# Two mixture-of-experts starts, the hand-over between experts, and the compressed attention branch, rearranged in one kernel

## The chip, the cores and the metric

The kernel runs on one core of one Trainium2 chip. The metric is the device time of one execution in microseconds (us). Most executions of one kernel agree within 0.3%.

Names: PE is TensorE (matmuls; PEld is its weight load), DVE is VectorE, ACT is ScalarE, POOL is GpSimd and SP is SyncE, whose queue issues the loads of weights. A name with a q (PEq, DVEq) is that engine's instruction queue.

## The reference, cut to what matters

Two transformer blocks of two layers each on 256 tokens of width 1024, all in f32. The first block has a gMLP and latent attention mixer, then an NSA mixer (native sparse attention), each followed by a hierarchical mixture of 32 experts (hidden width 256). The second block has two hybrid mixers, two cross attentions, one dense feed-forward and one mixture of 8 experts with hidden width 2816. The parts that matter here:

```python
def compress_kv(k, pos_emb, w1, w2):            # S=256 tokens, G=2 groups, D=64
    blocks = ...                                 # 15 blocks of 32 tokens, stride 16, + pos_emb
    return gelu(flat @ w1) @ w2                  # w1: 2048 x 256, w2: 256 x 64

def nsa_compressed(q, k_cmp, v_cmp):             # 16 heads, 8 of a group; 15 compressed keys
    s = einsum('btgid,bngd->bgitn', q, k_cmp) * D ** -0.5
    p = where(mask, softmax(where(mask, s, NEG)), 0.0)
    return einsum('bgitn,bngd->btgid', p, v_cmp)
# later: o = gates[0] * o_cmp + gates[1] * o_slc + gates[2] * o_win

def moe(x):                                      # top 2 of n experts for each token
    y = sum_e weight_e * (silu(x @ w_gate[e]) * (x @ w_up[e])) @ w_down[e]
```

## The kernel before, in words

**Weights.** SP loads all weights in the order of a plan into a ring of 9 tiles of 1 MB (`weight_ring`); a tile is asked for when the one nine before it was used (`ring.used`). Where a product needs more than one pass of rounded f32, a tile is split in two: ACT rounds it into one of three buffers (`weights_high`, `HIGHS = 3`), which takes one ACTIVATE of 128x2048, and DVE leaves the rest in the ring (`leave_low`, one TENSOR_TENSOR of 128x2048). PE then forms `high*high + high*low + low*high` (`three_products`, L129 to L131) or two products (L1887).

**Stages.** Every engine runs its own list, written out by hand. `join()` (L186) ends a stage: each engine drains, raises a semaphore and waits for the other three. Nothing behind a join starts before it.

**The NSA mixer** (`nsa_mixer`). `projection` runs ten products, the last four of them the queries. After the join DVE builds the blocks for keys and values (16 instructions, L1168) and the gate logits (L1174), PE multiplies them with `w1` (L1188), ACT takes the gelu (L1209), PE multiplies with `w2` (L1194, L1197, L1201), DVE copies the results to SBUF, and a join follows. Then come 32 score matmuls, one for each head and half of the tokens, each with 64 rows and 15 columns (L1234), the softmax on DVE and ACT (L1243 to L1260), and for each of four pairs of token half t and group g: 8 transposes (one for each head, 128x15), a copy of 15x1024 by DVE (L1291), 8 matmuls of 15 rows and 64 columns (L1280) and a multiplication with the gates (L1294). A join ends the branch.

**A mixture of experts** (`sparse_experts`, run three times: twice with 32 small experts, once with 8 large ones of 11 chunks each). `split_rows` splits the token rows into two buffers of `weights_high`. DVE makes the 0/1 matrix `G`, which also lies in `weights_high` (buffer 0), and the weighted one, `GW`. PE turns `G` (L2225), gathers the rows of all slots in 8 products k = 0..7 into the 8 banks of PSUM (L2233), and DVE takes the even and ACT the odd ones to SBUF (L2250, L2262). Then PE sums the weights of the slots (L2241, 16 matmuls of one column), DVE copies the sums (L2254), and a join follows. Only behind it does ACT round the first tile, since all three buffers of `weights_high` are in use before.

**Small experts** (`SmallExperts`). ACT and DVE run `scalar_step` and `vector_step` for x = -3, -2, ...; step x splits the second tile of expert x+2 and the first of x+3, and makes the two halves of the window of x+3 (the columns of its slots; L2014 on ACT, L2060 on DVE). PE's first product is L1887.

**Large experts** (`SplitExpert`). For each expert PE runs two first products (gate and up) for each chunk j and one down product; the hidden rows are turned (L1599), rounded by ACT (L1698) and left low by DVE (L1718) before the down product. ACT and DVE follow `order()`, whose `part(j)` is L1698 on ACT and L1718 on DVE. The end of an expert in both lists reads

```python
        self.order(lambda q: self.low(dve, q, i), combine, part,
                   lambda q: next_window and self.low(dve, q, i + 1))
        self.used(dve, self.p0 + self.down(self.chunks - 1), i)
        nc.vector.tensor_copy(self.rows[:, 512:], c.psum[:, 5, :])...
        if next_window:
            next_window()
            self.low(dve, self.up(0), i + 1)
```

where `next_window` makes the window of the next expert: 128x1024, L1680 on ACT and L1684 on DVE. PE turns the output rows (L1634) and starts the next expert when L1684 is done.

Of the kernel before, what the change touches and what calls it, by code (L numbers as in the profile page):

```python
# [1079 lines left out]
def nsa_mixer(c, cat, ctx, ahead):  # L1080
# [12 lines left out]
    hid = sb("hid", [P, 2, CMP_HID // P, NSA_G * NCMP])  # L1093
    w2 = sb("w2", [P, 2, CMP_HID // P, NSA_D])
    kc = sb("kc", [P, NSA_G * NCMP])
    vc = sb("vc", [NCMP, NSA_G, NSA_D])
# [4 lines left out]
    pcT = c.xT[0:NCMP].rearrange("p (a k) t -> p a (k t)", a=2).rearrange("p a (h q) -> p a h q", q=P)  # L1101
    sc = sb("sc", [P, TT, NSA_H, NCMP])
# [3 lines left out]
                    (w2[:, 0], k_tiles(arg["c_w_ck2"][0])), (w2[:, 1], k_tiles(arg["c_w_cv2"][0]))] +  # L1106
                [(pos[a * 64:(a + 1) * 64, i, :], posv[a, :, i, :]) for a in range(2) for i in range(2)])

    @c.block.gpsimd
    def _(pool):  # L1110

        nc.gpsimd.memset(ends[:, :, :], 0.0)
        nc.gpsimd.memset(block_rows[:, CMP_LEN * at_j:], 0.0)
        nc.gpsimd.memset(vs[:, :, NSA_KV:], 0.0)
        nc.gpsimd.memset(vwg[:, :, NSA_KV + 3 * NSA_H:], 0.0)
        c.pool(nc.gpsimd.memset(ends01[:, :, :], 1.0))
        pool.drain().then_inc(*c.sig("blocks_padded").up())
        for t in range(TT):
            for m, fill in ((ends, NEG), (ends01, 0.0)):
                nc.gpsimd.affine_select(out=m[:, t, :], in_=m[:, t, :], compare_op=ALU.is_ge, fill=fill,  # L1120
                                        base=t * P - CMP_LEN + 1, pattern=[[-CMP_STRIDE, NCMP]], channel_multiplier=1)
    w_in = arg["c_w_in"][0]
# [15 lines left out]
    def input_low(dve):  # L1138
        dve.wait_ge(*high.at(1))
        nc.vector.tensor_tensor(parts[1], c.xT[:, :, :], c.xh[:, :, :].bitcast(F32), ALU.subtract).then_inc(*c.sig("input_split").up())  # L1140
    projection(c, [
# [8 lines left out]
        Cols(parts, w_in, at(4), NSA_KV, "dve", spread(3, nc.vector.tensor_copy))] + [  # L1150
        Cols(parts, w_in, j * 256, 256, "dve" if j % 2 else "act",
             (dve_copy if j % 2 else act_copy)(qT[:, 2 * j:2 * j + 2, :])) for j in range(4)])
# [3 lines left out]
    built, hidden, squashed, compressed = c.sig("blocks_built"), c.sig("cmp_hidden"), c.sig("cmp_squashed"), c.sig("cmp_ready")  # L1156

    @c.block.vector
    def _(dve):
        dve.wait_ge(*c.sig("mixer_params_landed").now())  # L1160
        for i in range(2):
            for a in range(2):
                h = slice(a * 64, (a + 1) * 64)
                for g in range(NSA_G):
                    src = kvT[h, i, g, :].rearrange("p (m r) -> p r m", r=CMP_STRIDE)
                    for half in range(2):
                        js = slice(half * 8, half * 8 + 8)
                        last = nc.vector.tensor_tensor(  # L1168
                            blocks[h, i, js, g, :], src[:, a:CMP_STRIDE:2, half:half + NCMP],
                            pos[h, i, js].unsqueeze(2).broadcast_to([64, 8, NCMP]), ALU.add)  # L1170
            dve.drain().then_inc(*built.up())

        for t in range(TT):
            last = nc.vector.tensor_tensor(gates[:, t, :], vwg[:, t, NSA_KV:NSA_KV + 3 * NSA_H], gate_b[:, :], ALU.add)  # L1174
        dve.drain().then_inc(*built.up())

    @c.block.tensor
    def _(pe):
        pe.wait_ge(*c.sig("blocks_padded").now())
        pe.wait_ge(*c.sig("mixer_params_landed").now())  # L1180
        pe.wait_ge(*built.at(2))
# [11 lines left out]
        for m in range(2):  # L1193
            last = nc.tensor.matmul(c.psum[0:64, 4, 0:NSA_G * NCMP], w2[:, 0, m, :], hid[:, 0, m, :], start=(m == 0), stop=(m == 1))  # L1194
        last.then_inc(*compressed.up())
        for m in range(2):
            last = nc.tensor.matmul(c.psum[64:128, 5, 0:NSA_G * NCMP], w2[:, 0, m, :], hid[:, 0, m, :], start=(m == 0), stop=(m == 1))  # L1197
        last.then_inc(*compressed.up())
        for g in range(NSA_G):
            for m in range(2):  # L1200
                last = nc.tensor.matmul(c.psum[0:NCMP, 6 + g, 0:NSA_D], hid[:, 1, m, g * NCMP:(g + 1) * NCMP], w2[:, 1, m, :],  # L1201
                                        start=(m == 0), stop=(m == 1))
# [3 lines left out]
    def _(act):  # L1206
        act.wait_ge(c.ring.used, c.cmp_tile)
        for i in range(2):
            last = nc.scalar.activation(hid[:, i], c.psum[:, 2 * i:2 * i + 2, 0:NSA_G * NCMP], ACT.Gelu_apprx_tanh)  # L1209
# [3 lines left out]

    @c.block.vector
    def _(dve):
        dve.wait_ge(*compressed.at(3))
        nc.vector.tensor_copy(kc[0:64, :], c.psum[0:64, 4, 0:NSA_G * NCMP])
        nc.vector.tensor_copy(kc[64:128, :], c.psum[64:128, 5, 0:NSA_G * NCMP])
        for g in range(NSA_G):
            nc.vector.tensor_copy(vc[:, g, :], c.psum[0:NCMP, 6 + g, 0:NSA_D])  # L1220
    c.join()


    scored, softened = c.sig("cmp_scores"), c.sig("cmp_probs")
    exped = c.sig("cmp_exp")
    in_exp = c.sig("cmp_centred")

    @c.block.tensor
    def _(pe):
        for t in range(TT):  # L1230
            for h in range(NSA_H):
                g, a = h // NSA_HPG, h % 2
                rows = slice(a * 64, a * 64 + 64)
                last = nc.tensor.matmul(c.psum[:, 2 * a + t, (h // 2) * NCMP:(h // 2 + 1) * NCMP],  # L1234
                                        qT[rows, h // 2, t * P:(t + 1) * P], kc[rows, g * NCMP:(g + 1) * NCMP], start=True, stop=True)
        last.then_inc(*scored.up())

    @c.block.vector
    def _(dve):
        dve.wait_ge(*scored.at(1))  # L1240
        for t in range(TT):
            for a in range(2):
                nc.vector.scalar_tensor_tensor(  # L1243
                    sc[:, t, a:NSA_H:2, :], c.psum[:, 2 * a + t, 0:8 * NCMP].rearrange("p (h n) -> p h n", n=NCMP), NSA_D ** -0.5,
                    ends[:, t, :].unsqueeze(1).broadcast_to([P, 8, NCMP]), ALU.mult, ALU.add)
# [7 lines left out]
        c.dve(nc.vector.tensor_tensor(sc[:, :, :, :], sc[:, :, :, :], red[:, :, :].unsqueeze(3).broadcast_to([P, TT, NSA_H, NCMP]), ALU.mult))  # L1253
        nc.vector.tensor_tensor(sc[:, :, :, :], sc[:, :, :, :], ends01[:, :, :].unsqueeze(2).broadcast_to([P, TT, NSA_H, NCMP]),
                                ALU.mult).then_inc(*softened.up())
# [6 lines left out]
    turned, copied, out_ready, taken = c.sig("cmp_turned"), c.sig("cmp_copied"), c.sig("cmp_out"), c.sig("cmp_taken")  # L1262

    @c.block.tensor
    def _(pe):
        pe.wait_ge(*softened.at(1))
        for t in range(TT):
            for g in range(NSA_G):
                j = 2 * t + g
                if j >= 2:  # L1270
                    pe.wait_ge(*copied.at(j - 1))
                for i in range(NSA_HPG):
# [251 lines left out]
class SplitExpert:  # L1524
# [164 lines left out]
    def scalar(self, act, i, gate_squashed, next_window):  # L1689
# [11 lines left out]
        if next_window:  # L1701
            next_window()
# [1519 lines left out]
```

## Time and profile before

| what | value |
|---|---|
| time, median of 3 runs | 2651.18 us (2651.12 to 2653.88) |
| the profiled execution's own time | 2649.35 us |
| its span (first to last instruction) | 2647.6 us |
| mean granted TensorE clock | 0.939 |
| busy: PE, DVE, ACT | 2300.4, 1798.0, 1368.1 us |

The profile is of one execution. Its span leaves out 1.75 us that lie around it, and its own time is 1.83 us under the median of the runs. A busy time is the time in which an engine had an instruction under way; the chain that ended last is followed back from the last instruction to what released each one. The granted clock is 1.0 at TensorE's full 2.4 GHz and 0.5 at 1.2 GHz.

### The profile page before, as it was taken

Reading aid. Unit: us, or ns where it says so; the run is one execution under the profiler, and the core shown is the slowest. Engines: PE = TensorE matmul, PEld = TensorE weight load, DVE = VectorE, ACT = ScalarE, POOL = GpSimd, SP = SyncE. Lnnn points to the kernel's source line nnn. Section 1 sums busy time; section 2 is a strip of 40 time slices with the busy share of each in tenths; the row PEclk is TensorE's granted clock in tenths of the full one; section 3 lists DMA queues with packets and bytes.
Section 4 is the critical chain, followed back from the end, with each engine's and each line's share of the span. In section 5 each row is a group of like instructions: output and inputs, shape, how many; then the busy total and the mean of one; then the engine's idle time right before and its main releaser. Section 6 shows DMA issues by size and latency. Waiting matters only on the chain.

```text
span 2647.6 us, 43661 instructions
## 1 busy us (share of the span) xinstructions
PE 2300.4 (87%) x16404; PEld 2139.5 (81%) x16404; DVE 1798.0 (68%) x2101; ACT 1368.1 (52%) x1563; POOL 67.5 (3%) x111
## 2 busy tenths in 40 slices
PE   5568999788769999786889987777999999999997
PEld 4458999776569999775789877667999999998996
DVE  3457777434576765677456657646888888888886
ACT  3316556224345554444343344434777777777775
POOL 0010000000000000100000010000000000000000
PEclk8879999887889999898999999898999999999999
DMA  6227999460239998532345562333999999999993
GB/s 219 80 82 283 373 372 359 137 191 1 83 114 364 364 358 319 142 112 80 127 144 191 159 166 98 96 127 106 312 364 345 345 365 343 344 364 344 339 366 135
DMA packets 335529, 609.66 MB, mean 230 GB/s; under 512 B 11008, under 2 KB 266832, under 8 KB 310704
## 3 DMA queue, kind: packets, MB, share of 16 engines
q1 hardware_dynamic: 329696, 590.84, 63.9%
q0 software_dynamic: 5024, 13.16, 2.2%
q8 instruction: 185, 3.03, 0.5%
q10 hardware_dynamic: 560, 2.10, 0.2%
q14 instruction: 64, 0.52, 0.1%
HBM read 605.02 MB, written 1.05 MB: 229 GB/s over the span
## 4 chain that ended last, share of the span: by engine, by line
PE 77%; DVE 12%; ACT 4%; issue 3%; DVEq 2%; POOLq 1%; DMA 0%; ACTq 0%; POOL 0%; PEldq 0%
PE psum L129 16%; PE psum L131 16%; PE psum L130 16%; PE psum L1887 9%; PE psum L1923 9%; PE psum L1911 2%; DVE weight_ring_rounded L116 1%; PE psum L487 1%; DVE h_cf L2749 1%; ACT scores L760 1%; PE psum L2233 1%; PE psum L712 1%; PE psum L2420 1%; PE psum L548 1%; PE psum L309 1%
## 5 line engine op out<-in xcount | busy, mean ns | idle before, releaser
L1652 DVE TENSOR_TENSOR weight_ring_rounded<-weight_ring,weights_high_rounded 128x2048 fp32r<-128x2048 f32 x264 | 604.1, 2291 | 94.1 <-ACT weights_high_rounded L1647 93.9
L1647 ACT ACTIVATE weights_high_rounded<-weight_ring 128x2048 fp32r<-128x2048 f32 x264 | 504.7, 1915 | 105.4 <-PE psum L131 97.2
L129 PE MATMUL psum<-weights_high_rounded,scores_rounded 128*128 128x256 f32 x1408 | 406.2, 288 | 11.4 <-DVE scores_rounded L1684 10.5
L131 PE MATMUL psum<-weights_high_rounded,scores_rounded 128*128 128x256 f32 x1408 | 398.7, 283 | 0.0
L130 PE MATMUL psum<-weight_ring_rounded,scores_rounded 128*128 128x256 f32 x1408 | 398.4, 283 | 0.0
L1981 DVE TENSOR_TENSOR weight_ring_rounded<-weight_ring,weights_high_rounded 128x2048 fp32r<-128x2048 f32 x128 | 292.7, 2291 | 95.7 <-ACT weights_high_rounded L1976 95.7
L129 PEld LDWEIGHTS psum<-weights_high_rounded,scores_rounded 128*128 128x128 f32 x1408 | 270.0, 192 | 16.3 <-DVE scores_rounded L1684 12.1
L1887 PE MATMUL psum<-weights_high_rounded,scores_rounded 128*128 128x256 f32 x1024 | 263.7, 295 | 12.4 <-DVE scores_rounded L2060 10.7
L130 PEld LDWEIGHTS psum<-weight_ring_rounded,scores_rounded 128*128 128x128 f32 x1408 | 270.2, 192 | 3.4
L131 PEld LDWEIGHTS psum<-weights_high_rounded,scores_rounded 128*128 128x128 f32 x1408 | 270.0, 192 | 0.0
L131 PE MATMUL psum<-weights_high_rounded,xT_rounded 128*128 128x512 f32 (+3 forms) x688 | 261.5, 380 | 0.0
L1923 PE MATMUL psum<-xT_high,weight_ring 128*128 128x128 f32 x2048 | 241.6, 276 | 16.7 <-issue 12.3
L1887 PE MATMUL psum<-weight_ring_rounded,scores_rounded 128*128 128x256 f32 x1024 | 253.1, 285 | 0.0
L1923 PEld LDWEIGHTS psum<-xT_high,weight_ring 128*128 128x128 f32 x2048 | 234.6, 192 | 20.5 <-issue 15.8
L1976 ACT ACTIVATE weights_high_rounded<-weight_ring 128x2048 fp32r<-128x2048 f32 x128 | 243.7, 1905 | 3.2 <-POOLq L212 3.0
L129 PE MATMUL psum<-xT_high_rounded,weights_high_rounded 128*128 128x256 f32 x768 | 217.0, 283 | 14.8 <-DVE weight_ring_rounded L116 9.8
L116 DVE TENSOR_TENSOR weight_ring_rounded<-weight_ring,weights_high_rounded 128x2048 fp32r<-128x2048 f32 (+3 forms) x76 | 159.8, 2113 | 95.9 <-ACT weights_high_rounded L112 95.6
L131 PE MATMUL psum<-xT_high_rounded,weight_ring_rounded 128*128 128x256 f32 x768 | 215.5, 281 | 0.0
L1887 PEld LDWEIGHTS psum<-weights_high_rounded,scores_rounded 128*128 128x128 f32 x1024 | 197.7, 193 | 13.1 <-DVE scores_rounded L2060 10.9
L1887 PEld LDWEIGHTS psum<-weight_ring_rounded,scores_rounded 128*128 128x128 f32 x1024 | 198.2, 194 | 0.4 <-issue 0.4
L112 ACT ACTIVATE weights_high_rounded<-weight_ring 128x2048 fp32r<-128x2048 f32 (+3 forms) x76 | 133.8, 1768 | 117.4 <-PE psum L131 62.9
L130 PE MATMUL psum<-xT_rounded,weights_high_rounded 128*128 128x256 f32 x672 | 188.5, 281 | 0.0
(525 smaller groups left out, 4075.0 us busy)
## 6 DMA issues: line engine op xcount, KB each, us to landing
weight_ring<-in_moe_w_gate_dram SPq DMA_DIRECT2D x152, 1024.0 KB, 6.4
weight_ring<-in_moe_w_up_dram SPq DMA_DIRECT2D x152, 1024.0 KB, 8.4
weight_ring<-in_moe_w_down_dram SPq DMA_DIRECT2D x152, 1024.0 KB, 8.5
weight_ring<-in_w_in_dram SPq DMA_DIRECT2D x20, 1024.0 KB, 7.0
weight_ring<-in_ffn_w_gate_dram SPq DMA_DIRECT2D x11, 1024.0 KB, 5.4
weight_ring<-in_ffn_w_up_dram SPq DMA_DIRECT2D x11, 1024.0 KB, 5.3
weight_ring<-in_ffn_w_down_dram SPq DMA_DIRECT2D x11, 1024.0 KB, 4.9
weight_ring<-in_w_out_dram SPq DMA_DIRECT2D x8, 1024.0 KB, 5.0
```

Of the source, the lines that this page charges most:

```text
L112: self.ring.nc.scalar.activation(self.high, self.whole, ACT.Copy).then_inc(self.ring.high_ready, 1)
L116: self.ring.nc.vector.tensor_tensor(self.low, self.whole, self.high.bitcast(F32), ALU.subtract).then_inc(self.ring.split_ready, 1)
L129: nc.tensor.matmul(out, lh, rh, start=start, stop=False)
L130: nc.tensor.matmul(out, lh, rl, start=False, stop=False)
L131: return nc.tensor.matmul(out, ll, rh, start=False, stop=stop)
L1647: self.c.nc.scalar.activation(ring.high(self.s0 + q, 1, SLOT), ring.view(self.p0 + q, 1, SLOT), ACT.Copy).then_inc(ring.high_ready, 1)
L1652: self.c.nc.vector.tensor_tensor(ring.low(self.p0 + q, 1, SLOT), ring.view(self.p0 + q, 1, SLOT), ring.high(self.s0 + q, 1, SLOT).bitcast( ...
L1887: last = self.c.nc.tensor.matmul(psum[:, x % 2, a * CH:(a + 1) * CH], self.x[:, x % 2, k, :], w[:, k, :], start=(k == 0 and w is high), st ...
L1911: last = nc.tensor.matmul(psum[:, 2 + x % 2, at:at + self.W], blocks[:, a, m, :], self.twice, start=True, stop=True)
L1923: last = nc.tensor.matmul(psum[:, 4 + 2 * (x % 2) + k // 4, (k % 4) * P:(k % 4 + 1) * P], wt[:, m, k * P:(k + 1) * P], self.hidden[:, x % ...
L1976: self.c.nc.scalar.activation(ring.high(s, 1, SLOT), ring.view(self.gate_tile(x) + a, 1, SLOT), ACT.Copy).then_inc(ring.high_ready, 1)
L1981: self.c.nc.vector.tensor_tensor(ring.low(tile, 1, SLOT), ring.view(tile, 1, SLOT), ring.high(s, 1, SLOT).bitcast(F32), ALU.subtract).then ...
```

## The change

It has four parts.

1. **Compressed branch.** The blocks are built inside the projection, as steps on DVE ahead of query products 0 and 2, and the gate logits behind the last; the join behind the projection is gone, and so is the one ahead of the scores. The gelu of the values is written eight times side by side (`hid_stack`, 8x15 columns for each group), so that the value product yields 120 rows, which DVE multiplies with a mask (`own_block`) into a block-diagonal `vc` of 120x512 for each group. `kc` holds, for each group, the keys of two heads side by side in 128 columns padded with zeros, so that one matmul of 128 rows and 128 columns scores two heads (16 matmuls in all). The gates and the mask are folded into the reciprocal of the softmax (two operations on 128x32), and the last multiplication is done in two halves. Four transposes (128x120), two copies of 120x256 and four matmuls of 120 rows and 512 columns replace the four rounds; ACT copies one half of the output and DVE the other.
2. **Start of the experts.** `split_rows` uses `c.S_rounded` in place of two buffers of `weights_high`, and `G` moves to the buffer that the third tile will want. ACT and DVE split the first two tiles between their copies of the gathered rows. ACT copies k = 1, 3, 4, 5, 7 and DVE 0, 2, 6.
3. **Slot sums.** The 16 matmuls and the copy move behind the join, into bank 7; DVE takes the sums after its half of the first window.
4. **Hand-over of large experts.** `next_window()` is called in `order()` ahead of the last `part(j)` on both engines, in place of after the expert's last down product (DVE) or after the split of the next gate tile (ACT).

```diff
+        Cols(parts, w_in, at(4), NSA_KV, "dve", spread(3, nc.vector.tensor_copy)),
+        build(0), queries[0], queries[1], build(1), queries[2], queries[3], Step("dve", gate_logits)], join=False)
...
-        pe.wait_ge(*built.at(2))
+        pe.wait_ge(*built.at(3))
...
+        nc.scalar.activation(hid[:, :, :], c.psum[:, 0:2, 0:NSA_G * NCMP], ACT.Gelu_apprx_tanh)
+        for m in range(2):
+            nc.scalar.activation(hid_stack[:, m].rearrange("p g (h n) -> p g h n", n=NCMP), ..., ACT.Gelu_apprx_tanh)
...
+            for p in range(NSA_H // 2):
+                last = nc.tensor.matmul(c.psum[:, t, 2 * p * NCMP:2 * p * NCMP + P], qT[:, p, t * P:(t + 1) * P],
+                                        kc[:, 2 * p // NSA_HPG, :], start=True, stop=True)
...
+        for t in range(TT):
+            pe.wait_ge(*copied.at(t + 1))
+            for g in range(NSA_G):
+                nc.tensor.matmul(c.psum[:, 2 * t + g, :], pcT[:, t, g, :], vc[:, g].rearrange("p h d -> p (h d)"),
+                                 start=True, stop=True).then_inc(*out_ready.up())
...
         for j in range(self.chunks):
+            if j == last and next_window:
+                next_window()
             part(j)
             if j == last:
                 next_split(self.gate(0))
...
-    high, low = flat(1), flat(2)
+    high, low = (c.S_rounded[:, a, :, :].rearrange(...) for a in range(2))
...
-    G = c.ring.highs[:, 0, 0:TT * SLOTS].rearrange("p (t s) -> p t s", t=TT)
+    G = c.ring.highs[:, (len(ring.split_tiles) + 2) % HIGHS, 0:TT * SLOTS].rearrange("p (t s) -> p t s", t=TT)
...
+        first_high(act, 0)
+        for k in (1, 3, 4, 5, 7):
+            act.wait_ge(*gathered.at(k + 1))
+            nc.scalar.activation(xg[:, k, 0:SLOTS], c.psum[:, k, :], ACT.Copy)
+            if k == 1:
+                first_high(act, 1)
...
+        for k in (0, 2, 6):
+            dve.wait_ge(*gathered.at(k + 1))
+            nc.vector.tensor_copy(xg[:, k, 0:SLOTS], c.psum[:, k, :])
+            if k < 6:
+                first_low(dve, k // 2)
+    c.join()
+    # PE: the slot sums, into c.psum[:, 7, ...]
+    # DVE: take_slot_weights behind the first window
```

## Rows read from the trace of the kernel before

**Rows 1.** The page: busy time, share of the span and instructions of each engine.
```profile
PE 2300.4 (87%) x16404; PEld 2139.5 (81%) x16404; DVE 1798.0 (68%) x2101; ACT 1368.1 (52%) x1563; POOL 67.5 (3%) x111
```
**Rows 2.** The chain that ended last, compressed branch: start us, us, what.
```profile
564.50 16.84 PE psum L1188 x128
...
583.82 4.73 PE psum L1234 x64
...
592.59 0.67 DVE c_sc L1253
...
594.00 1.90 PE psum L1273 x8
...
621.28 0.69 DVE c_oc L1294
```
**Rows 3.** Windows: us, busy by engine, granted clock, DMA share, GB/s.
```profile
564.50:567.00 2.50, 2.50 (x12) 2.50 (x13) 0.16 (x2) 0.00 (x0) 0.00 (x0) 0.50 0.00 0
...
571.00:575.00 4.00, 4.00 (x38) 4.00 (x37) 0.00 (x0) 0.00 (x0) 0.00 (x0) 1.00 0.78 264
...
612.00:622.00 10.00, 7.93 (x36) 6.77 (x35) 2.59 (x3) 0.00 (x0) 0.00 (x0) 0.50 0.00 0
```
**Rows 4.** Timeline of DVE ahead of the compressed branch.
```profile
547.15 0.69 DVE L1124 COPY c_qT<-psum 128x512 f32<-128x512 f32 x1 [0.95 <-PE psum L131]
558.51 0.69 DVE L1124 COPY c_qT<-psum 128x512 f32<-128x512 f32 x1 [10.67 <-PE psum L131]
559.53 4.68 DVE L1168 TENSOR_TENSOR c_blocks<-c_kvT,c_pos 64x120 f32<-64x120 f32 x16 [0.34 <-POOLq L212]
```
**Rows 5.** Groups of PE by shape: busy us, mean ns of one.
```profile
L548 PE MATMUL psum<-weight_ring,ab_lowT 128*128 128x512 f32 x16 | 7.3, 599 | 1.5 <-POOLq L212 1.5
```
**Rows 6.** Timeline of a small-expert start.
```profile
197.40 1.84 PE L2241 MATMUL psum<-ones,e_outT 128*128 128x1 f32 x16
197.60 0.60 ACT L2262 ACTIVATE e_xg<-psum 128x512 f32<-128x512 f32 x1 [1.35 <-PE psum L2233]
...
199.72 1.91 ACT L1976 ACTIVATE weights_high_rounded<-weight_ring 128x2048 fp32r<-128x2048 f32 x1 [1.52 <-POOLq L212]
...
201.53 0.61 ACT L2014 ACTIVATE scores_rounded<-e_xg 128x512 fp32r x1
...
203.87 0.68 DVE L2060 TENSOR_TENSOR scores_rounded<-e_xg,scores_rounded 128x512 fp32r<-128x512 f32 x1
...
204.61 0.58 PE L1887 MATMUL psum<-weights_high_rounded,scores_rounded 128*128 128x256 f32 x1 [5.37 <-DVE scores_rounded L2060]
```
**Rows 7.** Timeline of the large-expert start.
```profile
1818.28 0.60 ACT L2262 ACTIVATE e_xg<-psum 128x512 f32<-128x512 f32 x1 [1.21 <-PE psum L2233]
...
1822.76 1.04 ACT L1680 ACTIVATE scores_rounded<-e_xg 128x1024 fp32r x1
...
1826.37 0.58 PE L129 MATMUL psum<-weights_high_rounded,scores_rounded 128*128 128x256 f32 x1 [6.45 <-DVE scores_rounded L1684]
```
**Rows 8.** Windows around that start (columns as in rows 3).
```profile
1821.00:1822.00 1.00, 0.00 (x0) 0.00 (x0) 0.00 (x0) 1.00 (x1) 0.00 (x0) 1.00 0.03 8
...
1829.00:1832.00 3.00, 3.00 (x16) 3.00 (x15) 1.72 (x1) 0.06 (x1) 0.00 (x0) 0.50 0.00 0
1832.00:1834.00 2.00, 2.00 (x18) 2.00 (x17) 0.00 (x0) 1.99 (x3) 0.00 (x0) 0.94 0.35 75
```
**Rows 9.** Timelines of one hand-over between large experts.
```profile
1922.32 0.42 DVE L1718 TENSOR_TENSOR xT_rounded<-psum,xT_rounded 128x256 fp32r<-128x256 f32 x1
...
1922.88 0.47 PE L129 MATMUL psum<-weights_high_rounded,xT_rounded 128*128 128x512 f32 x1 [0.18 <-DVE xT_rounded L1718]
...
1926.57 1.21 DVE L1684 TENSOR_TENSOR scores_rounded<-e_xg,scores_rounded 128x1024 fp32r<-128x1024 f32 x1
...
1927.84 0.38 PE L129 MATMUL psum<-weights_high_rounded,scores_rounded 128*128 128x256 f32 x1 [0.47 <-DVE scores_rounded L1684]
```
**Rows 10.** Window in the stream of small experts (columns as in rows 3).
```profile
230.00:290.00 60.00, 58.15 (x499) 57.63 (x498) 42.37 (x36) 35.64 (x42) 0.00 (x0) 1.00 0.95 367
```

More of the change, by code:

```diff
@@ L1193, in _ @@
         for m in range(2):
[L1194 to L1197, printed above, removed]
+            last = nc.tensor.matmul(c.psum[:, 4, 0:NSA_G * NCMP], w2k[:, m, :], hid[:, m, :],
+                                    start=(m == 0), stop=(m == 1))
         last.then_inc(*compressed.up())
@@ L1218, in _ @@
-        nc.vector.tensor_copy(kc[64:128, :], c.psum[64:128, 5, 0:NSA_G * NCMP])
-        for g in range(NSA_G):
[L1220 to L1226, printed above, removed]
+        dve.wait_ge(*c.sig("masks_ready").now())
+        dve.wait_ge(*compressed.at(1))
+        for a in range(2):
+            h = slice(a * 64, a * 64 + 64)
+            nc.vector.tensor_copy(kc[h, :, a * NCMP:(a + 1) * NCMP], c.psum[h, 4, 0:NSA_G * NCMP].rearrange("p (g n) -> p g n", g=NSA_G))
@@ L1228, in _ @@
+        dve.drain().then_inc(*keyed.up())
+        dve.wait_ge(*compressed.at(2))
+        for g in range(NSA_G):
+            nc.vector.tensor_tensor(vc[:, g], c.psum[0:stack, 6 + g, 0:NSA_D].unsqueeze(1).broadcast_to([stack, NSA_HPG, NSA_D]),
+                                    own_block[0:stack, :].unsqueeze(2).broadcast_to([stack, NSA_HPG, NSA_D]), ALU.mult)
+        dve.drain().then_inc(*valued.up())
     @c.block.tensor
     def _(pe):
+        pe.wait_ge(*keyed.at(1))
         for t in range(TT):
[L1231 to L1235, printed above, removed]
@@ L1296, in nsa_mixer @@
+        for t in range(TT):
+            dve.wait_ge(*out_ready.at(2 * t + 2))
+            nc.vector.tensor_copy(oc[:, t, 512:], c.psum[:, 2 * t + 1, :]).then_inc(*taken_dve.up())
     c.join()
@@ L1655, with order @@
     EARLY = 2
-    def order(self, split, squash, part, next_split):
+    def order(self, split, squash, part, next_split, next_window):
         last = self.chunks - 1
@@ L2106, in split_rows @@
     nc = c.nc
-    flat = lambda a: c.ring.highs[:, a, :].rearrange("p (t d) -> p t d", t=TT)
-    high, low = flat(1), flat(2)
+    high, low = (c.S_rounded[:, a, :, :].rearrange("p k t -> p (k t)").rearrange("p (t d) -> p t d", t=TT) for a in range(2))
     rounded = c.sig("rows_high")
@@ L2331, in sparse_experts, with first_high, first_low, _ @@
         way = SplitExpert(c, p0, per, chunks, xg, squashed, hidden, outT, landed, used)
+    def first_high(act, a):
+        small.high(act, 0, a, 0) if ahead else way.high(act, a, 0)
+    def first_low(dve, a):
+        small.low(dve, 0, a, 0) if ahead else way.low(dve, a, 0)
+    @c.block.scalar
+    def _(act):
+        act.wait_ge(*spread_turned.now())
+        nc.scalar.activation(spread[:, 0:2, :].rearrange("p s t -> p (s t)"), c.psum[:, 6, :], ACT.Copy).then_inc(spread_act.sem, 1)
+        first_high(act, 0)
[4 more added lines that the diff above has]
+                first_high(act, 1)
+    @c.block.vector
+    def _(dve):
+        dve.wait_ge(*spread_turned.now())
+        nc.vector.tensor_copy(spread[:, 2:4, :].rearrange("p s t -> p (s t)"), c.psum[:, 7, :]).then_inc(spread_dve.sem, 1)
+        for k in (0, 2, 6):
[4 more added lines that the diff above has]
+    c.join()
+    @c.block.tensor
+    def _(pe):
+        pe.wait_ge(*weighed.now())
+        for s in range(SLOTS // P):
+            ss = slice(s * P, (s + 1) * P)
+            for t in range(TT):
+                last = nc.tensor.matmul(c.psum[:, 7, s:s + 1], GW[:, t, ss], c.ones[:, 0:1], start=(t == 0), stop=(t == TT - 1))
+        last.then_inc(*slots_summed.up())
+    def take_slot_weights(dve):
+        dve.wait_ge(*slots_summed.now())
+        nc.vector.tensor_copy(slot_w[:, :], c.psum[:, 7, 0:SLOTS // P])
     def small_streams():
```

206 lines of the change are left out of this document (92 added, 114 removed).

## The prediction

> **What bounds the kernel now.** I read the page first: PE is busy for 87% of the span and nothing else comes near [rows 1]. So a part of the change is worth what it takes from PE's idle time, from work on PE, or from the time in which PE runs at half its clock. I then read the chain of waits, which alternates between PE and whatever PE waits for, and made timelines and windows of the places that the diff touches. They are four: the compressed branch (558 to 622 us), the start of the two streams of small experts (198 and 761 us, alike), the start of the large ones (1818 us), and the seven hand-overs between large experts. Everywhere else the work is the same, and moves as a whole.
>
> In the compressed branch PE waits 6 us for the blocks, and then the chain is serial: every term is transposes, a copy, matmuls, in turn [rows 2, 4]. PE runs at half clock both at its start and at its end [rows 3]. At the expert starts PE has nothing from the slot sums to its first product, 5.37 and 6.45 us, and starts at half clock [rows 6 to 8]. At a hand-over PE stands 0.18 us for L1718 and 0.47 us for L1684 [rows 9].
>
> **Part 1, compressed branch.** Six terms.
>
> Start. Now: DVE's last query copy ends at 559.20, the 16 block instructions take 4.68 us, PE starts L1188 at 564.50 [rows 2, 4]. After: only the gate logits (two small operations, some 0.35) stand behind that copy, so PE starts at about 559.75: **-4.75**. The blocks go in two halves of 2.34 us into the projection. The second lies in the 10.67 us in which DVE waits for PE after 547.84. The first comes at 540.5, when DVE has two tiles left to split (2.3 each). Its cover: the third query product starts at about 547.1 [rows 4], and 540.5 + 2.34 + 2.3 is 545.2. If that cover is gone, it costs up to 2.3. Behind this step wait the splits and two copies of queries on DVE, and PE for them.
>
> Clock. At the start of L1188 the granted clock is 0.50, and 12 records take 2.5 us where later 38 take 4.0 [rows 3]. Half clock lasts from 564.5 to about 569.3, so full clock would save 2.4. PE's pause shrinks from 6.0 to 1.3 us. At the large start the clock is still 1.00 2 us into a pause [rows 8]. I take **-2.4**; the other bound is 0.
>
> Gelu to softmax. L1188 ends at 581.34, the scores start at 583.82, 2.48 later [rows 2]. After: three gelu instructions in place of two (two of them 240 wide; nearest row 0.60 for 512, so 0.8 in all), key product, two small copies, no join: about 2.0, **-0.5**. The value product and its two masked copies (0.69 each, as a 128x512 copy [rows 4]) lie beside the scores. The scores are 32 records of 128 columns in place of 64 of 15: at the 38 in 4.0 us of [rows 3] they take 3.4 to 3.6 in place of 4.73; at half clock 7. I take 3.55, and half of DVE's scaling runs beside them, 0.3: **-1.5**; the other bound +2.3.
>
> Behind the reciprocal. Two operations of 0.67 and the start of PE make 1.4 (592.59 to 594.00) [rows 2]. After: two tiny ones (0.2 each) and half of one (0.37): 0.8, **-0.6**.
>
> The rounds. From 594.00 to the end of L1294, 621.97: 27.97 [rows 2]. After: the first two transposes at the 0.24 of L1273 (8 in 1.90), 0.5; copy of 120x256, 0.45; four matmuls of 512 columns; a copy of 0.69. Such a matmul is two records. The nearest row has 16 records in 7.3 us, 0.456 each, some at either clock [rows 5]: four matmuls 3.65. PE comes here out of a pause of 4 us, so I take half clock at first: bounds 3.4 and 6.8, value 6.3. The sum is 0.5 + 0.45 + 6.3 + 0.69 and 0.1 of waits, 8.0: **-20**; bounds -19.4 and -22.8.
>
> Attention behind it starts at half clock now [rows 3] and would find PE just after 6 us of dense work: **-0.5**, bounds 0 and -3.
>
> Part 1 together: **-30.2**.
>
> **Parts 2 and 3, starts.** Small experts: the last copy ends at 198.20, but PE's slot sums (1.84) and DVE's copy hold the join to 199.6; then ACT rounds a whole tile (1.91), makes its half of the window (0.61), DVE takes the tile (2.29) and its half of the window (0.68), and PE starts at 204.61 [rows 6]. After: the join passes at 198.45; the offset is read (0.5), then 0.61 and 0.68 with small gaps, and PE starts at about 200.4. The slot sums end at 198.5 + 1.84, 200.35: just hidden; if PE takes them later, it costs their 1.84 at most. That is -4.2. The splits fit between the copies: ACT's at 189.8 to 191.7 and 192.3 to 194.2, DVE's at 191.9 to 194.2 and 194.9 to 197.2, its copy of k = 6 behind them to 197.9; ACT's last copy, 198.20, still ends the stage. If this cover is gone (a copy that comes late), DVE's end moves by what it is late beyond 0.3. PE's pause shrinks to under 1 us, and its first 16 matmuls, which took 3.46, would take 1.95 at full clock: -1.4. Each start **-5.6**, two **-11.2**.
>
> Large experts, by the same steps: last copy 1818.88, join, 0.6 to the window, 1.04 and 1.21 in place of two tiles more, PE at 1822.1 for 1826.37 [rows 7]: -4.3. There PE ran at half clock to 1832, at 16 records in 3.00 where 18 then took 2.00 [rows 8]: -2.8 more. **-7.1**. The rows and G in other buffers are read by the same instructions: 0.
>
> **Part 4, hand-over.** This speaks against the change. DVE is in order: the last up product, `combine`, the split of the last down tile, then `part` (L1718) at 1922.32 with no idle ahead of it. PE waits for just this L1718, 0.18 us [rows 9]. After, DVE's window half (1.21) stands ahead of it. PE's last down product so starts 1.13 to 1.21 later. What is won: L1684 is gone from the end, where PE stood 0.47. The split of the next gate tile that DVE now does 1.2 later is still done well before PE wants it; ACT's half runs in a pause of ACT. So each hand-over costs 1.13 - 0.47, **+0.66**, seven times **+4.6**; bounds: +3.3 (all 0.65 of idle won) and +5.5.
>
> **Sum.** -30.2 - 11.2 - 7.1 + 4.6 = -43.9. The profiled execution took 2649.35 around its span of 2647.6; the median is 1.83 above it. 2651.18 - 43.9 = **2607.3**.
>
> **Rivals.** (a) PE's clock stays low at the four starts although the pauses shrink: 2.4 + 2.8 + 2.8 = 8.0 are not won, 2615.3. For it: PE's only work there are one-column matmuls or none. Against: the clock still held in [rows 8].
> (b) The window half is hidden after all and the 0.47 is won seven times: -3.3 in place of +4.6, 2599.4. Against it stands PE's wait for L1718 [rows 9].
> (c) The pause of 1.3 us that part 4 makes ahead of every last down product drops the clock. A phase like that of the large start costs 2.8, seven times 20: 2627. The skill's section HAM oscillation (same page) describes such a loop, bursts parted by waits, in which the clock falls in each turn. [...] Against it in the rows: full clock 2 us into a pause [rows 8]; no row here shows a fall behind so short a one.
> (d) The blocks inside the projection delay PE by both halves: +4.7, 2612.
> (e) The change does not do what it says in the small streams, since loads bound them: the DMA share is 0.95 there [rows 10]. The 11.2 would be given back at the end of each stream, 2618.5. Against it: SP asks for a tile when another is used, so the loads start earlier as well.
> (f) Slower than before: the mechanism of (c), with a clock that then stays low. 43.9 must be eaten beyond the 4.6 already counted, 6.3 for each of seven, which takes a half-clock phase of over 12.5 us after each; at 99 us for an expert that is an eighth of it. The rows know one so long, the branch up to 622 [rows 3], but with PE sparsely used.
>
> **How the numbers follow.** Forecast as summed, 2602 to 2613: 0.62. (a) 0.12, (b) 0.07, (c) 0.04, (d) 0.05, (e) 0.05, (f) 0.01, no change at all 0.01, others 0.03. The range 2599 to 2620 holds the forecast, (a), (b), (d) and (e) and leaves out (c), (f) and the rest, with tails somewhat over a tenth. 0.2%, about what a measurement can tell here from no change, is 5.3 us: all cases but the last few are faster by more. Faster 0.97, same 0.01, slower 0.02.
>
> **What the profile after would show.** PE's L1188 group starts 1.3 us behind the last query product and takes 14.3 us; from the first transposes of the probabilities to the next stage some 8 to 9 us in place of 28. PE's first expert product comes 4.3 us earlier after the gather, with clock 1.00. At each hand-over the wait of the first down matmul for L1718 grows from 0.18 to about 1.3, and the wait for L1684 is gone. I am wrong if that wait stays small, if clock 0.50 follows it, or if the DVE wait for the parameters or a split in the projection shows up ahead of the query products.

## The result, and the profile after

The changed kernel takes 2625.91 us (median of 4 executions, 2614.12 to 2627.8), beside 2652.53 for the kernel before on the same chip. The ratio is 0.9887, 95% interval 0.9857 to 0.9916. A second, larger comparison gave 0.9875 (0.9856 to 0.9894), 33 us. I forecast 43.9 us less, 2607.3, with a range of 2599 to 2620. The sign was right, the size was not, and the time lies outside the range.

The profiled execution is the shortest of these, 2614.12 us with a span of 2612.2. Of its page, busy time by engine, to set against [rows 1]:

```profile
PE 2276.5 (87%) x16284; PEld 2115.4 (81%) x16284; DVE 1791.5 (69%) x2094; ACT 1371.7 (53%) x1569; POOL 68.7 (3%) x116
```

PE lost 23.9 us of busy time and the span 35.4, so 11.5 us of idle time went as well. Line numbers have moved: L1188 is now L1206, L1234 is L1257, L2241 is L2355, L1887 is L1904, L1718 is L1736, L1684 is L1704, L1722 is L1740.

The chain through the compressed branch, to set against [rows 2]:

```profile
557.12 14.54 PE psum L1206 x128
571.68 0.22 ACT c_hid L1224
571.90 0.56 ACTq L1229
...
574.00 3.64 PE psum L1257 x32
...
582.16 0.70 PE psum L1290 x2
...
582.88 0.43 DVE xT L1310
...
583.45 5.48 PE psum L1297 x8
...
588.96 0.69 DVE c_oc L1313
```

From the first transposes to the end of the last copy it is 7.5 us, where it was 27.97. The blocks are built inside the projection; DVE's timeline ahead of the branch, to set against [rows 4]:

```profile
538.04 2.39 DVE L1168 TENSOR_TENSOR c_blocks<-c_kvT,c_pos 64x120 f32<-64x120 f32 x8
540.55 4.49 DVE L116 TENSOR_TENSOR weight_ring_rounded<-weight_ring,weights_high_rounded 128x2048 fp32r<-128x2048 f32 x2
545.07 0.69 DVE L1136 COPY c_qT<-psum 128x512 f32<-128x512 f32 x1
545.86 2.37 DVE L1168 TENSOR_TENSOR c_blocks<-c_kvT,c_pos 64x120 f32<-64x120 f32 x8
555.80 0.69 DVE L1136 COPY c_qT<-psum 128x512 f32<-128x512 f32 x1 [7.57 <-PE psum L131]
```

DVE still waits 7.57 us for PE there, so PE was not held up by the blocks.

The first small start on PE's timeline, to set against [rows 6]:

```profile
199.13 1.95 PE L2355 MATMUL psum<-ones,e_outT 128*128 128x1 f32 x16 [0.91 <-POOLq L212]
201.56 0.58 PE L1904 MATMUL psum<-weights_high_rounded,scores_rounded 128*128 128x256 f32 x1 [0.49 <-DVE scores_rounded L2079]
201.95 0.42 PE L1904 MATMUL psum<-weight_ring_rounded,scores_rounded 128*128 128x256 f32 x1
```

Windows of that start (columns as in [rows 3]):

```profile
200.00:202.00 2.00, 1.51 (x12) 1.43 (x12) 0.76 (x2) 2.00 (x2) 0.00 (x0) 0.84 0.02 4
202.00:204.00 2.00, 2.00 (x11) 2.00 (x11) 1.60 (x1) 0.89 (x2) 0.00 (x0) 0.50 0.03 8
```

PE is idle for only 1.4 us between the gather and its first product, yet the clock falls to 0.50 at the first product, as before the change. The second small start is alike, with pauses of 0.91 and 0.24 us. At the large start the second pause is longer:

```profile
1782.22 1.95 PE L2355 MATMUL psum<-ones,f_outT 128*128 128x1 f32 x16 [0.91 <-POOLq L212]
1785.68 0.58 PE L129 MATMUL psum<-weights_high_rounded,scores_rounded 128*128 128x256 f32 x1 [1.51 <-DVE scores_rounded L1704]
```

From 1785 to 1788 the mean clock is 0.53. Last, DVE's timeline at a hand-over, to set against [rows 9]:

```profile
1880.54 1.22 DVE L1704 TENSOR_TENSOR scores_rounded<-e_xg,scores_rounded 128x1024 fp32r<-128x1024 f32 x1
1881.67 0.42 DVE L1736 TENSOR_TENSOR xT_rounded<-psum,xT_rounded 128x256 fp32r<-128x256 f32 x1
```

PE's timeline there:

```profile
1882.23 0.47 PE L129 MATMUL psum<-weights_high_rounded,xT_rounded 128*128 128x512 f32 x1 [1.31 <-DVE xT_rounded L1736]
...
1886.05 0.66 PE L1652 MATMUL psum<-ident,xT 128*128 128x128 f32 x4 [0.35 <-DVE xT L1740]
1887.16 0.36 PE L129 MATMUL psum<-weights_high_rounded,scores_rounded 128*128 128x256 f32 x1 [0.45 <-issue]
```

The wait of the last down product grew from 0.18 to 1.31, as forecast. The wait for the window is gone, but the first product of the next expert still starts 0.45 us late, now with no releaser named ("issue"). Over the seven hand-overs this last pause is 0.45 to 0.66 us; before the change, where it stood as a wait for the window, it was 0.47 to 0.66.

Single executions of one kernel scatter here by more than the usual 0.3%: 42 of the kernel before, over all comparisons, lie between 2649.8 and 2662.0 (median 2655.9), 13 of the changed one between 2614.0 and 2629.3 (median 2624.0). So I took more profiles of both, and set stage by stage the means of four against four. The borders are starts of PE instructions (gather, last matmul of the last down product of a stream, L712, first L129, last row transpose of an expert) and DVE's last query copy.

| stage | before, us | after, us | difference | forecast |
|---|---|---|---|---|
| gather 1 to last down product, stream 1 | 300.3 (296.7 to 303.5) | 295.4 (293.9 to 297.9) | -4.9 | -5.6 |
| last query copy to attention | 63.8 | 34.3 (34.0 to 34.5) | -29.5 | -30.2 |
| attention to gather 2 | 130.2 | 130.5 (129.0 to 132.0) | +0.4 | |
| gather 2 to last down product, stream 2 | 297.7 (296.7 to 299.1) | 293.3 (292.6 to 294.7) | -4.4 | -5.6 |
| gather 3 to first large product | 16.6 | 12.9 | -3.65 | -4.3 |
| first large expert | 100.99 | 101.04 | +0.04 | -2.8 and +0.66 |
| the next six | 594.5 | 600.3 | +5.8 | +4.0 |
| all other stages | 1148.5 | 1149.4 | +1.0 | 0 |
| span | 2652.5 | 2617.2 | -35.3 | -43.9 |

The forecast of the branch holds its 0.5 for the attention. Over the four profiles each, the two streams with their starts scatter so much that the standard error of their summed difference, 9.3, is 2.3 us; that of the span's is 3.2.

### The profile page after: what moved, and what is told of

The parts are those of the page before. It is cut to its first block, busy times and chain, and to the rows that moved or that the text cites. A ratio compares the mean times of both kernels' runs of the same rounds, so it can differ in the third digit from the quotient of the medians.

```text
span 2612.2 us, 43413 instructions
## 1 busy us (share of the span) xinstructions
PE 2276.5 (87%) x16284; PEld 2115.4 (81%) x16284; DVE 1791.5 (69%) x2094; ACT 1371.7 (53%) x1569; POOL 68.7 (3%) x116
## 4 chain that ended last, share of the span: by engine, by line
PE 78%; DVE 12%; ACT 4%; issue 3%; DVEq 2%; POOLq 1%; DMA 0%; ACTq 0%; POOL 0%; PEldq 0%
PE psum L129 17%; PE psum L131 16%; PE psum L130 16%; PE psum L1904 9%; PE psum L1940 9%; PE psum L1928 2%; DVE weight_ring_rounded L116 1%; PE psum L487 1%; DVE h_cf L2775 1%; ACT scores L760 1%; PE psum L2253 1%; PE psum L2446 1%; PE psum L548 1%; PE psum L1617 1%; PE psum L712 1%
## 5 line engine op out<-in xcount | busy, mean ns | idle before, releaser
L129 PE MATMUL psum<-weights_high_rounded,scores_rounded 128*128 128x256 f32 x1408 | 405.4, 288 | 5.2 <-issue 3.7
L129 PEld LDWEIGHTS psum<-weights_high_rounded,scores_rounded 128*128 128x128 f32 x1408 | 269.4, 191 | 10.1 <-issue 5.2
L1904 PE MATMUL psum<-weights_high_rounded,scores_rounded 128*128 128x256 f32 x1024 | 262.8, 294 | 2.6 <-DVE weight_ring_rounded L1998 1.4
L1904 PE MATMUL psum<-weight_ring_rounded,scores_rounded 128*128 128x256 f32 x1024 | 252.1, 284 | 0.0
L129 PE MATMUL psum<-xT_high_rounded,weights_high_rounded 128*128 128x256 f32 x768 | 216.6, 282 | 14.8 <-DVE weight_ring_rounded L116 9.8
L1904 PEld LDWEIGHTS psum<-weights_high_rounded,scores_rounded 128*128 128x128 f32 x1024 | 196.9, 192 | 4.0 <-DVE weight_ring_rounded L1998 1.7
L1904 PEld LDWEIGHTS psum<-weight_ring_rounded,scores_rounded 128*128 128x128 f32 x1024 | 197.4, 193 | 0.0
```

The source lines that it names most:

```text
L129: nc.tensor.matmul(out, lh, rh, start=start, stop=False)
L1904: last = self.c.nc.tensor.matmul(psum[:, x % 2, a * CH:(a + 1) * CH], self.x[:, x % 2, k, :], w[:, k, :], start=(k == 0 and w is high), st ...
```

## Experiments

**The changed kernel again.** No edit.

> The changed kernel as it is, once more. The profiled execution of it took 2614.1 us, the others 2624.8 to 2627.8 at a mean granted clock lower by 0.005. If the clock falls behind the 1.3 us pauses of the hand-overs in the usual execution (theory P, the pause), a profile at 2625 shows clock 0.50 behind some last down products, and expert periods over 100 us. If the clock falls elsewhere (theory E, elsewhere), the seven periods are the 100.1 of the first profile, and one long half-clock stretch of some 20 us is found in another stage.

Median 2620.01 of 6 (2613.96 to 2629.29). The profile (span 2617.0) has hand-over periods, counted from the last row transpose of one large expert to that of the next, of 99.97 to 100.11, and no low clock among the large experts behind the first start: nothing for theory P. Theory E's single stretch of some 20 us is not there either. The span is 4.8 us longer than in the first profile, and of this 1.3 lie ahead of gather 1, 1.8 between the first stream and the last query copy, and 1.4 between the second stream and gather 3.

**Without part 4.** In `order` the call goes, and the window stands behind again, on both engines (ACT's lines are shown):
```
-            if j == last and next_window:
-                next_window()
...
+        if next_window:
+            next_window()
```

> The changed kernel without its part 4: the window of the next large expert stands behind the last steps again. The profiles give 1.05 us for each of seven hand-overs, so both theories expect 7 us less in the profiled execution. Theory P (the pause drops the clock in the usual execution) expects the gap between executions to go as well: 2607, 18 us less than the changed kernel's median. Theory E expects the gap to stay: some 2618 for the usual execution.

Median 2610.90, ratio 0.9836 (0.9823 to 0.9849). The first large expert takes 99.91, the next five 98.87 to 98.98 and the one behind them 99.53, where PE waits 0.24 us more for a split tile. Beside the changed kernel's profiles, part 4 costs 1.1 us for the first hand-over and 1.0 on average for each of the others. The median lies between the 2607 of theory P and the 2618 of theory E and does not decide between them.

**The window behind the last part**, ahead of the next split:
```
             part(j)
+            if j == last and next_window:
+                next_window()
             if j == last:
```

> The window of the next expert right behind the last hidden part, ahead of the split of the next gate tile: the last down product does not wait for it, and it is still done over 2 us before the first product. Theory of the hand-over as in the changed kernel's profile: the pause before the last down product falls from 1.31 to 0.2 us and the 0.45 us of PE's own queue at the first product stays, so 1.05 to 1.1 us less for each of seven, 7 to 8 less than the changed kernel, the same as with the window late to within 2 us.

This expectation failed: 2624.49, ratio 0.9889 (0.9875 to 0.9903), no better than the changed kernel. DVE's timeline at a hand-over of this kernel:

```profile
1886.86 1.23 DVE L1704 TENSOR_TENSOR scores_rounded<-e_xg,scores_rounded 128x1024 fp32r<-128x1024 f32 x1
1888.56 2.29 DVE L1670 TENSOR_TENSOR weight_ring_rounded<-weight_ring,weights_high_rounded 128x2048 fp32r<-128x2048 f32 x1 [0.47 <-ACT weights_high_rounded L1665]
1890.76 0.69 DVE L1740 COPY xT<-psum 128x512 f32<-128x512 f32 x1
```

PE's timeline there:

```profile
1886.86 0.47 PE L129 MATMUL psum<-weights_high_rounded,xT_rounded 128*128 128x512 f32 x1 [0.18 <-DVE xT_rounded L1736]
...
1891.51 0.66 PE L1652 MATMUL psum<-ident,xT 128*128 128x128 f32 x4 [1.17 <-DVE xT L1740]
1892.62 0.36 PE L129 MATMUL psum<-weights_high_rounded,scores_rounded 128*128 128x256 f32 x1 [0.45 <-issue]
```

The last down product no longer waits. But ACT and DVE now split the next gate tile later, DVE's copy of the rows stands behind that split, and PE waits 1.17 us for the copy where it waited 0.35. The price has only moved. Besides, this kernel has low clock behind three of the seven hand-overs, although the pauses are alike at all seven; two windows of it, ahead of the first product and behind it:

```profile
1890.00:1893.00 3.00, 1.38 (x11) 0.93 (x9) 3.00 (x3) 2.73 (x2) 0.00 (x0) 1.00 0.94 318
1893.00:1896.00 3.00, 3.00 (x18) 3.00 (x18) 3.00 (x3) 0.00 (x0) 0.00 (x0) 0.56 1.10 363
```

Its periods are 101.16, 101.26 and 101.36 where that happens, 99.77 to 99.88 where not: 1.4 us each.

**Part 4 alone**, on the kernel before (the same lines of `order`, `scalar` and `vector` as in the diff).

> Part 4 alone, on the kernel before. My forecast for it was +4.6 us (seven times 0.66); the profile after shows +1.05 for each, so +7.4: 2658.5. Theory P expects more in the usual execution, up to +20: 2671.

Median 2664.07, ratio 1.0027 (1.0015 to 1.0039): +7.2 us, where 7.4 was expected. Periods of 99.98 to 100.12.

**Part 1 alone**, the diff's hunks in the NSA mixer, on the kernel before.

> Part 1 (the compressed branch) alone, on the kernel before. My forecast for it was -30.2 us; the profile after has the stretch from the last query copy to the attention at 34.15 us for 63.8, so -29.6. If the parts add up, the ratio is 0.9888. If the branch's gain is partly lost later, for example to a colder clock in the attention behind it, the ratio is above 0.990.

Median 2627.68, ratio 0.9892 (0.9875 to 0.9909): -28.7 us.

**Parts 2 and 3 alone**, the diff's hunks in the sparse experts without part 4, on the kernel before.

> Parts 2 and 3 (the expert starts) alone, on the kernel before. My forecast was -18.3 us, with full clock at the starts. The profile after shows -3.7, -4.0 and -3.65 at the three starts, and some 1 us of clock at the large one: -12.4 if the streams keep it, ratio 0.9953. If the streams of small experts are bound by their loads and give their part back at their ends (rival e), only the large start is left: -4.7, ratio 0.998.

Median 2645.34, ratio 0.9949 (0.993 to 0.9968): -13.5 us. The product of the three ratios is 0.9868, that of the whole 0.9875 (0.9856 to 0.9894): the parts add up within the intervals.

**Slot sums 128 columns wide**, window late:
```
-  matmul(c.psum[:, 7, s:s + 1], GW[:, t, ss], c.ones[:, 0:1], ...
+  matmul(c.psum[:, 7, ss], GW[:, t, ss], c.ones[:, :], ...
-  tensor_copy(slot_w[:, :], c.psum[:, 7, 0:SLOTS // P])
+  tensor_copy(slot_w[:, :], c.psum[:, 7, 0:SLOTS:P])
```

> The changed kernel with the window late again, and with each slot sum written 128 columns wide in place of 1, which takes the same 1.9 us of PE. The first expert products behind them start at half clock in every profile so far. If what PE does in those 1.9 us decides (columns), the 16 first products take 1.95 us in place of 3.6 and the clock's low step is gone from all three starts, 1.7 us each, so 2 to 5 us less than the run with the window late (2611). If the pause of 0.9 us ahead of the sums decides, nothing changes.

Median 2610.13, ratio 0.9837 (0.9816 to 0.9859). PE's timeline at the first start:

```profile
199.28 2.05 PE L2356 MATMUL psum<-ones,e_outT 128*128 128x128 f32 x16 [0.92 <-POOLq L212]
201.72 0.39 PE L1905 MATMUL psum<-weights_high_rounded,scores_rounded 128*128 128x256 f32 x1 [0.39 <-DVE scores_rounded L2080]
201.94 0.28 PE L1905 MATMUL psum<-weight_ring_rounded,scores_rounded 128*128 128x256 f32 x1
```

A window of it:

```profile
202.00:204.00 2.00, 2.00 (x19) 2.00 (x19) 1.45 (x1) 1.08 (x3) 0.00 (x0) 1.00 0.01 4
```

The pauses are nearly the same, 0.92 and 0.39 us for 0.91 and 0.49, and the sums take 2.05 us for 1.95. Now the clock is 1.00 at this start and at the other two; at the large one the pauses are 0.91 and 1.40 us for 0.91 and 1.51. The 16 first products of a small start take 2.2 us, where every kernel with narrow sums needs 3.4 to 3.8, and the first large expert takes 98.64 for 99.91. The expected 2 to 5 us less than with the window late did not show in the median of this run: it is 0.8 less.

**Only half of each down tile loaded** in the small experts. This kernel leaves out part of the computation, with the same instructions:
```
-  tile(p0 + 2 + 3 * x + (2 if x + 1 < n else 0), down(e, 0))
+  tile(p0 + 2 + 3 * x + (2 if x + 1 < n else 0), down(e, 0)[:, 0:1, :])
-  wt[:, m, k * P:(k + 1) * P]
+  wt[:, 0, k * P:(k + 1) * P]
```

> The changed kernel with only the first half of every small expert's down tile loaded (the down products use that half twice, so part of the computation is left out, and the instructions are the same). In the streams most experts take 8.3 us, and every fourth or fifth 9 to 11, some 23 us more in a stream than 31 times 8.33. If the loads make these long ones and the scatter between executions, both streams fall to about 260 us from 283, the median falls by 40 to 46 us against the changed kernel, and the executions lie within 5 us instead of 15. If something else makes them (instruction fetch, the widths of experts), the periods stay as they are.

Median 2608.29, ratio 0.9817: some 16 us less than the changed kernel, and not 40 to 46. The two streams, from their first products, fell to 276.9 and 276.0 from 283.3 and 280.9 in the first profile after, not to 260. The 5 executions lie within 6.1 us (2603.91 to 2610.04) where 13 of the changed kernel spread over 15.3. That does not show that the loads make the scatter: kernels with all their loads spread over 5.8 (window behind the last part, four executions), 7.5 (window late, five) and 14.9 (wide slot sums, five). A row of the waits of the changed kernel (us in total, times, longest):

```profile
PE psum L1940 <- issue: 15.2, 17, 2.1
```

The same of this kernel:

```profile
PE psum L1940 <- issue: 7.3, 8, 1.7
```

PE's waits ahead of a down product are halved. The 260 was a mistake of mine: it left out the first expert's 13 us ahead of its down product. With them, 12 and 10 us were to be won, and about half of that came.

**Two more profiles of the changed kernel.**

> The changed kernel, one more profiled execution, to see where its longer executions lose time. Profiled so far: 2612.2 and 2617.0 us of span; unprofiled ones reach 2627. If the loads of the two streams make the difference (theory S), the hand-over periods are again 100.0 to 100.2 and the two streams with their starts add up to 586 us in a short execution and 595 or more in a long one. If the pauses of part 4 do (theory P), single hand-over periods are 101.3 or more, with the clock at 0.50 behind the last down product.

2624.02 us.

> The same as the look before it, for a second sample: theory S expects normal hand-overs and streams of 586 to 598 us that rank with the span; theory P expects periods of 101.3 or more.

2619.76 us. In all four profiles (spans 2612.2 to 2622.0) the six periods behind the first large expert are 99.96 to 100.19, so theory P, the falling clock at the hand-overs, has no support. Theory S holds in part. Streams with their starts add up to 588, 589, 591 and 587 us, the longest in the longest execution, but over a range of 4 us where the spans have 10. The rest lies in the other stages: attention to gather 2 takes 129.1, 129.0, 132.0 and 132.0, at a mean clock of 0.90, 0.90, 0.87 and 0.87, and the stages of the table's last row but one take 1146.8, 1151.2, 1149.9 and 1150.1.

**Wide slot sums and window late, once more side by side.**

> Slot sums 128 columns wide and the window late, beside the same kernel with the sums of one column. The first profile had full clock at all three starts and the first large expert 1.27 us shorter; in the streams the loads may give the 1.7 us of each start back. So 1.3 us less if given back, 4.5 us less if kept; either is near the limit of what five rounds can tell.

Median 2607.74, ratio 0.9825 (0.9802 to 0.9848).

> The changed kernel with the window late, beside the dense sums on the same chip: ratio to the kernel before 0.983 to 0.985 again, as in its first run (0.9836).

Median 2616.54, ratio 0.9843 (0.9821 to 0.9866). Over both runs, ten executions each, the medians are 2608.9 with wide sums and 2612.9 with narrow ones. The difference of the means is 3.0 with a standard error of 2.3, from the scatter: likely, not shown. What is shown is the clock at the starts, the 16 first products of each small one and the 1.3 us of the first large expert.

The narrow one's profile holds the longest second stream of all kernels with the new starts (301.7 us from its gather) and shows a part of how one arises. PE's timeline at one of its down products:

```profile
826.75 0.98 PE L1941 MATMUL psum<-xT_high,weight_ring 128*128 128x128 f32 x3 [2.99 <-issue]
```

A window from there:

```profile
826.00:834.00 8.00, 7.25 (x39) 7.28 (x40) 3.55 (x4) 0.92 (x3) 0.00 (x0) 0.58 0.67 267
```

Behind a wait of 2.99 us the mean clock over 8 us is 0.58, so such a wait is paid twice.

**Three more profiles of the kernel before**, for the table above.

> The kernel before, profiled again. Its first profile (2649.35 us) lies at the low end of 38 executions with a median of 2655.7; this one should be near 2655. If the streams of small experts explain it, both with their starts add up to about 600 us in place of 593.9 and the other stages stay within 1 us. If the clock's luck in the middle stages does, the stretches between the streams and the gathers grow instead.

2656.81 us.

> The same, a second sample: 600 us for both streams with their starts, 267 to 269 from the first stream to the second gather, hand-over periods of 98.9 to 99.1.

2660.24 us.

> The same, a third sample. With the three, the stages' means of the kernel before can be set against those of the four profiles of the changed one; I expect a difference of 9 to 12 us in the streams with their starts, 31 in the branch, 4.7 at the large start, 7.5 the other way in the hand-overs.

2650.60 us. The two streams with their starts are 600.5, 602.6 and 595.1 us long, against 593.9 in the profile that the forecast was made from: that profile showed the streams at their shortest. Any other row of the table agrees within 1 us, and the rest of the stages together within 3. Of the differences that I expected, the streams (9.3 for 9 to 12) and the large start (4.7) came out; the branch is at 29.5 for 31 and the hand-overs at 6.9 for 7.5.

## Why the prediction was wrong

The miss of 18.6 us, 2625.91 for 2607.3, has three pieces by the medians: 4.7, 12.0 and 1.9. The part that the sum itself got wrong is the second. Two steps of it failed in their mechanism: that the clock would hold at the expert starts, and that a hand-over would win back the 0.47 us of its second wait.

**The base: 4.7 us.** I subtracted from 2651.18, the median of three executions. Over 42 it is 2655.9. That an execution of this kernel varies by 12 us was not in my range at all.

**The sum: 12.0 us by the medians** (31.9 won for 43.9), 8.6 by the stage table. Step by step, with the table:

- *Part 1, forecast -30.2, measured -29.5 (timed alone -28.7).* The mechanism and nearly every term were right. The start came 1.35 us behind the last query product, L1206 ran 14.54 us at full clock, the rounds took 7.5 us for 8.0 (their eight records 5.48 for 6.3, at a mean clock of 0.66 from 583 to 589), the attention starts at clock 1.00. Two terms were off: gelu to scores took 2.3 for 2.0, with 0.56 in ACT's queue, and the attention up to gather 2 gained nothing (130.5 for 130.2).
- *Starts of the small experts, forecast -5.6 each, measured -4.9 and -4.4.* In the means of four the product starts 3.7 and 3.8 us earlier for the 4.2 forecast: the join passes at 199.1 and not at 198.45. The rest of each difference is within the scatter of the streams, and so is their shortfall of 1.9.
- *The clock at the starts, forecast 1.4, 1.4 and 2.8.* This step failed. I wrote that PE's pause shrinks to under 1 us and so the clock holds. The pauses did shrink, to 0.91 and 0.49 (at the large start 1.51), and PE still starts at 0.50; the 16 first products take 3.5 to 3.7 us and not 1.95. The rival (a), to which I gave a chance of 0.12, is right for the three expert starts and wrong for the branch. At the large start 1.1 of my 2.8 came, since the low clock lasts shorter: 99.91 for 100.99, both without part 4. The runs with wide sums show what I missed: the forecast counts the slot sums as work that keeps the clock. With 128 columns in 2.05 us it is kept, with one column in 1.95 us it is not. (The step also has a slip: 3.46 less 1.95 is 1.5, not 1.4.)
- *Large start itself, forecast -4.3, measured -3.65.*
- *Part 4, forecast +4.6, measured +6.9 (timed alone +7.2).* The new wait was sized right, 1.31 for 0.18. What failed is "what is won": 0.47 for L1684. With that wait gone, the first product is kept back 0.45 us all the same. In the code, PE reads the expert's count and branches there (`by_width`); that this is what takes the time is argued, the trace names no releaser. Two waits lay side by side, and the trace of before shows only the one that ended last. So 0.02 is won, and a hand-over costs about 1.0 to 1.1. My bounds of +3.3 and +5.5 left out the case that nothing is won, which by the same rows is seven times 1.13, 7.9.

The shortfalls are 1.1 (branch and attention), 1.9 (small starts), 2.4 (the large start and its clock), 2.3 (part 4) and 1.0 in stages that the change does not touch: together 8.7, with rounding the 8.6. Clear of the scatter are those of the large start, of its clock and of part 4.

**The sample, the rest.** The median of the first four executions was 1.9 above the changed kernel's usual one. Between the 8.6 of the table and the 12 of the medians some 3 us stay unlocated; they are within the scatter of four profiles.

The other rivals. (b) fell with the 1.31. (c), the clock falling behind the pause of each hand-over, would have given 2627, next to the measured median, but for the wrong reason: no profile of the changed kernel shows such a fall. The Trainium skill, "TensorE: Matmul & The Clock Gate", HAM oscillation, tells of such a pattern, bursts of matmuls parted by waits behind each of which the clock is low again, but with waits longer than these. The kernel with the window behind the last part shows a fall, behind three of seven hand-overs and at 1.4 us each. Its pauses (0.18, 1.17 and 0.45 to 0.69 us) are alike at all seven and add up to less than the changed kernel's (1.31, 0.35 and 0.45 to 0.66), behind which it never fell; what decides stays open. (d) fell: DVE still waited 7.57 us for PE ahead of the last query copy, not PE for DVE. (e), the gain given back at the end of the streams, fell too: they keep 9.3 of 11.2. The loads do matter there, but by about 6 us a stream when a sixth of the bytes is left out. (f) fell: the change is faster.

What makes the single waits in the streams is only argued. I went through one stream each in the first profile after, in that of the half loads and in the second with the window late: 17 waits over 0.4 us for which the trace names no releaser. In 15 a packet of the instruction queue begins 3.3 to 3.4 us before PE goes on, in the other two 2.3, and in none does a down tile land in the 3 us ahead. That points to PE's own code, fetched between the loads. But an up tile lands within 1.2 us in most of them too, and no run here separates the two.

**The better version.** The changed kernel with the window late and wide slot sums took 2610.13 and 2607.74 us, ratios 0.9837 and 0.9825 to the kernel before: some 12 us less than the changed kernel by the ratios. Part 4 is 9 of them by the ratios, 7 by the stages of the profiles.

## What to carry to other kernels

Before you count the end of a wait as won, ask what else the waiting engine has to do at that place: a trace names only the releaser that came last, and here 0.45 of 0.47 us stayed. An instruction of 1.2 us had no free place on DVE at these hand-overs: of the three places tried, the one where its wait showed was the cheapest. When a forecast rests on one execution, get the scatter of the base first, and make the range at least as wide.

## Unexpected of the hardware

The 16 slot sums of one column in 1.95 us, with pauses of 0.91 us ahead of them and 0.49 (small start) or 1.51 us (large start) behind, left the granted clock at 0.50 (1.2 GHz) for the products behind them. The same 16 with 128 columns in 2.05 us, with pauses of 0.92 and 0.39 or 0.91 and 1.40 us, left it at 1.00 (2.4 GHz), at all three starts and in both profiles. A busy PE in the profile is thus not the same as a PE that keeps its clock.

Leaving out a sixth of the bytes of the small experts' streams shortened each by only 5 to 6 us of some 280, although their DMA share is 0.95 [rows 10].
